# A pause of GpSimd at the end of a convolution block, and chunks of a normed input moved from ScalarE to VectorE

## What is computed

```
mod = silu(c) @ mod_w[layer] + mod_b[layer]          # 6 x 1024 columns
sh_m, sc_m, gt_m, sh_f, sc_f, gt_f = split(mod, 6)
h = x * (1 + sc_m) + sh_m                            # "normed input", modulated
y = concat(s5(h @ w_in), gla(h @ w_in)) @ w_out      # mixing block
x = layer_norm(ALPHA * x + (1 + gt_m) * y)
h = x * (1 + sc_f) + sh_f
f = swiglu(h)   (layer 0)   or   top-2 of 8 experts (layer 1)
x = layer_norm(ALPHA * x + (1 + gt_f) * f)
```

## Time and profile before

| | us |
|---|---|
| median of 3 runs | 2672.69 |
| lowest, highest | 2669.34, 2675.71 |
| the profiled execution | 2669.51 |
| its span in the profile | 2667.7 |

### The profile page before, as it was taken

How to read it: one execution, slowest core, us unless ns; L and a number is a source line. 1 busy time by engine, 2 the same in 40 slices (tenths; PEclk the granted TensorE clock), 3 DMA queues, 4 the chain that set the end, 5 groups by cost and what they waited for, 6 DMA issues and landing times. The chain is left out here.

```text
span 2667.7 us, 41694 instructions
## 1 busy us (share of the span) xinstructions
PE 2547.6 (95%) x15530; PEld 2223.3 (83%) x15530; DVE 2078.8 (78%) x2194; ACT 1495.0 (56%) x1786; POOL 902.1 (34%) x564
## 2 busy tenths in 40 slices
PE   8999899999998999988999887999999999999997
PEld 7999689999997999767999766888888888888885
DVE  6777666676788766787565787898989898989897
ACT  4336543343344343554343555777777777777775
POOL 6990069969859986023470020000000000000000
PEclk9999999999998999899999898999999999999999
DMA  8764357667656664325555325999999999999995
GB/s 304 258 236 157 113 213 258 230 215 257 236 203 228 226 211 166 123 88 189 182 180 182 119 92 215 350 360 333 366 341 359 347 353 353 351 353 351 349 345 187
DMA packets 214166, 665.31 MB, mean 249 GB/s; under 512 B 14640, under 2 KB 14960, under 8 KB 193952
## 3 DMA queue, kind: packets, MB, share of 16 engines
q1 hardware_dynamic: 196752, 602.62, 62.5%
q0 software_dynamic: 17296, 61.06, 6.7%
HBM read 662.58 MB, written 1.05 MB: 249 GB/s over the span
## 5 line engine op out<-in xcount | busy, mean ns | idle before, releaser
L1827 PE MATMUL work<-xT_hi,wh_gu 128*128 128x256 f32 x2088 | 595.3, 285 | 19.2 <-DVE xT_lo L1056 11.7
L1828 PE MATMUL work<-xT_lo,wh_gu 128*128 128x256 f32 x2088 | 593.3, 284 | 0.0
L1829 PE MATMUL work<-xT_hi,wl_gu 128*128 128x256 f32 x2088 | 592.7, 284 | 0.0
L924 DVE TENSOR_TENSOR wl_gu<-raw_gu,wh_gu 128x2048 fp32r<-128x2048 f32 x158 | 390.0, 2468 | 84.8 <-ACT wh_gu L407 84.4
L1827 PEld LDWEIGHTS work<-xT_hi,wh_gu 128*128 128x128 f32 x2088 | 402.5, 193 | 26.9 <-issue 20.8
L1828 PEld LDWEIGHTS work<-xT_lo,wh_gu 128*128 128x128 f32 x2088 | 402.9, 193 | 4.5
L1829 PEld LDWEIGHTS work<-xT_hi,wl_gu 128*128 128x128 f32 x2088 | 402.7, 193 | 0.0
L929 DVE TENSOR_TENSOR wl_d<-raw_d,wh_d 128x1024 fp32r<-128x1024 f32 x157 | 236.8, 1509 | 180.4 <-ACT wh_d L414 180.4
L1827 PE MATMUL acc<-wh_d,h_hi 128*128 128x512 f32 x912 | 371.5, 407 | 3.4 <-DVE h_lo L1529 2.7
L1828 PE MATMUL acc<-wl_d,h_hi 128*128 128x512 f32 x912 | 359.8, 395 | 0.0
L1829 PE MATMUL acc<-wh_d,h_lo 128*128 128x512 f32 x912 | 359.0, 394 | 0.0
(11 more groups left out here) (465 smaller groups left out, 4623.8 us busy)
## 6 DMA issues: line engine op xcount, KB each, us to landing
raw_gu<-in_w_gu SPq DMA_DIRECT2D x269, 1024.0 KB, 5.9
raw_d<-in_w_d SPq DMA_DIRECT2D x269, 512.0 KB, 5.2
scratch<-in_w_gu SPq DMA_DIRECT2D x112, 1024.0 KB, 7.5
scratch<-in_w_d SPq DMA_DIRECT2D x112, 512.0 KB, 6.7
scratch<-in_w_mod POOLq DMA_DIRECT2D x96, 512.0 KB, 3.6
rows<-in_norm_post POOLq DMA_DIRECT2D x6, 512.0 KB, 4.5
rows<-in_ln_g POOLq DMA_DIRECT2D x4, 512.0 KB, 4.3
rows<-in_ln_b POOLq DMA_DIRECT2D x4, 512.0 KB, 7.3
```

What stands on the lines that cost most here:

```text
L924: TT(wl, raw_gu[k][:, :], wh.bitcast(F32), ALU.subtract).then_inc(gu_lo, 1)
L1827: pe.matmul(out_, w[0], m[0], start=start, stop=False)
L1828: pe.matmul(out_, w[0], m[1], start=False, stop=False)
L1829: return pe.matmul(out_, w[1], m[0], start=False, stop=stop)
```

## The change

Three edits. GpSimd, in the fourth quarter of the modulation, waits before the 13th of its 24 steps until block 4 is done. In blocks 6, 7 and 8 chunk 1 is modulated by VectorE and no longer by ScalarE. The counts on `xt_f` and `xt_raw`, now three chunks each in a block, follow in ScalarE's `high` and in TensorE's waits of the last block; the last block itself keeps its shares (ScalarE 0, 1, 2 and 4, VectorE 3 and 5).

```diff
                 def high(j):
...
-                    if j in (3, 5):
-                        act.wait_ge(xt_raw, 2 * c + j // 2)
-                    else:
-                        act.wait_ge(xt_f, 4 * c + (1, 2, 3, 0, 4, 0)[j])
+                    act.wait_ge(xt_raw if j % 2 else xt_f, 3 * c + j // 2 + 1)
...
-                for j in (0, 1):
-                    modulated(j)
+                modulated(0)
                 if b == len(SUBS) - 1:
+                    modulated(1)
                     modulated(2)
                     modulated(4)
                     return
@@ gpsimd, modulation(i)
                     pool.wait_ge(mod_in[n % 3], 16 * (8 * i + n // 3 + 1))
+                    if i == 3 and n == 12:
+                        pool.wait_ge(x_done, SECOND - 1)
@@ tensor, moe(b)
-                    pe.wait_ge(xt_f, 4 * (b - SECOND) + (4 if t else 2))
+                    pe.wait_ge(xt_f, 3 * (b - SECOND) + (4 if t else 2))
                     if t:
-                        pe.wait_ge(xt_raw, 2 * (b - SECOND + 1))
+                        pe.wait_ge(xt_raw, 3 * (b - SECOND) + 2)
```

## The result

| | before | after |
|---|---|---|
| median of 22 runs each | 2674.22 us | 2676.74 us |
| lowest to highest | 2668.41 to 2678.44 | 2673.73 to 2680.78 |
| ratio of after to before, 95% interval | | 1.0015 (1.0008 to 1.0022) |
| the profiled execution | 2669.51 | 2677.67 |
| its span in the profile | 2667.7 | 2675.9 |

By the ratio the change costs 4 us (2 to 6); the two medians are 2.5 us apart. Either is less than the 0.2% that I had named as the least that can be told, though with this many runs its sign is clear. In the profile of after, lines of GpSimd, VectorE and ScalarE have numbers two or three lower than before (1094 for 1096, 1709 for 1711, 1758 is the same); TensorE's are the same.

What follows compares the result with a forecast made beforehand. TensorE, busy in 95% of the span, was taken to bound the kernel, with time won only in gaps between blocks. +7.2 us for block 5 and -3.2 us for three starts gave +4.0 on 2672.69: 2676.7 us, range 2668 to 2683.

Steps and rivals of the forecast that it cites:

- pause, end of block 4: End of block 4: VectorE's additions run undisturbed by GpSimd, so block 5's first matmul comes 2.4 us earlier (2.1 to 2.9).
- start of TensorE's turning of B, against before: Block 5: TensorE waits 7.7 us for B's loads and turns B at about 956.0 instead of 950.75, +5.3 us.
- clock behind the stand: Block 5, after TensorE's wait for B: 3 to 4.8 us at half speed, costing 1.9 us (1.4 to 2.4).
- three starts: Starts of blocks 6 to 8: with chunk 1 on VectorE, TensorE starts 1.07 us earlier each time, -3.2 us together.
- clock in blocks 6 to 8: First matmuls of these blocks run at half clock; where that ends decides the gain, -1.6 to -6 us.
- that may return: End of block 4: the diagonal can meet GpSimd's first product and lose about 0.8 us, partly hidden behind ScalarE's table load.
- GpSimd's delay: Modulation's fourth quarter: step 13 starts 8.0 us later, the last twelve steps take 86.2 us, the quarter ends 7.1 us later.
- The landing of B: Block 5: the last of B's eight transfers, issued at 949.2, lands 6.5 us later, at 955.7; ends 3.4 and 7.8 us.
- The stand of 3 us by the page's figure: Block 5: by the Trainium skill's fit alone, B is there at 951.4 and TensorE idles about 3 us.
- Line 1932: TensorE's next wait, at 1002.9: has room, everything later by the same 7 us within 2; a gap there would disprove the forecast.
- long stand: Rival, block 5: GpSimd needs 88.0 us, B takes 7.8 us, TensorE turns B at 959.1; +7.0 us, 2679.7; chance 0.20.

## Why the prediction came out, and what in it was wrong

I forecast 2676.7 us, and the median is 2676.74. That close a hit is luck: the terms were off by 0.6 to 1.4 us each, with both signs; the kernel before has a median of 2674.22 over 22 runs and not the 2672.69 of the three that I added to; and 2.1 us in the block of experts are in no term of mine. What the runs bear out is the mechanism, and a difference of 2 to 6 us.

| term | predicted | in the trace |
|---|---|---|
| pause, end of block 4 (contained in the next) | -2.4 | -1.84 |
| start of TensorE's turning of B, against before | +5.3 | +6.7 |
| clock behind the stand | +1.9 | +3.0 |
| three starts | -3.2 | -4.1 |
| clock in blocks 6 to 8 | in the range | -1.3 |
| sum | +4.0 | +4.3 |

- **The pause.** Right in its mechanism, but it left out TensorE's clock. Counted from block 4's last matmul, ScalarE's table load starts 2.87 us earlier (6.63 us for 9.50), which is what the additions had lost (2.89). Then ScalarE waits 0.51 + 0.56 us for turnings that run at the lower clock for 5.0 us, where it had waited 0.15, and 1.84 us arrive. The value lies under my lower bound of 2.1 by 0.3. The 0.8 us "that may return" with the diagonal did return in large part (0.95 us beside GpSimd's product, undisturbed 0.29), hidden behind the table load.
- **GpSimd's delay.** The best step: last twelve steps 86.2 us predicted, 86.2 measured. The last load of B was predicted at 949.2, or 951.2 with the 2.0 us by which this execution ran late; it was 951.1.
- **The landing of B.** I took 6.5 us, between 3.4 and 7.8, since the weight loads should be still. It was 8.3, outside both ends. This is the term that was sized worst. Those loads weren't still when the stand began: the DMA engines were full all through it (1.03), and the 512 KB of the gain stood ahead (B first: 6.7 us). With fewer weight loads beside it, in the run with the pause before step 12, the last landed in 4.3. The Trainium skill's DMA: Bandwidth & Descriptors, section "Anatomy of one DMA — SWDGE (gpsimd) path", by whose fit 64 KB take 2.2 us (an estimate from it: 2.0 us plus the bytes over 436 GB/s), agrees with the first load of B when nothing of GpSimd's is queued ahead of it (2.1 us, B ahead of the gain), and is far off for the last of eight under load. The stand of 3 us by the page's figure didn't come.
- **The start of the turning** is the sum of both: 959.44 - 2.0 - 950.75 = +6.7 us. It makes a stand of 8.09 us, predicted 7.7, TensorE having come later than I had it.
- **The clock.** I counted 3 to 4.8 us at half speed from a row in block 8; it was six. I took the row's 4.0 us as the whole, when it only says that the clock was at 0.50 up to its end (it came back at about 1581.4, after 4.4 us). Nor does the length of the stand tell it: behind stands of 5.93, 7.32, 8.09 and 12.46 us the clock stayed at 0.50 for 4.5, 3.3, 6.0 and 5.2 us. What sets it no run here shows; the six us of after are the longest of the four.
- **The chunks.** Sized too low by a third. I had put VectorE 0.2 us behind ScalarE; in the trace it is VectorE that waits 0.20 for ScalarE, and `low(2)` starts 1.32 us earlier, relative to ScalarE's first piece, not 1.07. The clock gave 1.3 us more, within my bounds, though part of that is the trace: with the old shares, too, the clock stayed low at the start of block 6 for 5.3 us in before and for 3.0 with the pause alone.
- **Line 1932** shows no wait of its own in after, as expected.

The errors add up to +1.4 + 1.1 - 0.9 - 1.3 = +0.3 us; by the lengths of whole blocks (+9.46 - 4.1 - 1.3) the sum is +4.1, and with the block of experts +6.2, the upper end of what the times allow. None of the rivals came true, though the "long stand" was nearest in the landing (7.8); it had GpSimd's end wrong (88.0 us for 86.2).

## What to carry to other kernels

A pause that takes one engine out of another's way can make everything behind it late; before making it, find the last load issued by that engine and how long before use it lands. Here that margin was 0.8 us, the pause made the loads 7 us late, and moving the reader by one pass of a loop, which by itself cost nothing (1.0001), made the difference between 1.0015 and 0.9969. Two edits in one change should be timed apart: this one hid a gain of 0.23% under a loss of 0.33%.

## What the runs showed of the hardware

- VectorE's addition to the residual took 3.23 us beside an addition of GpSimd's, 2.23 where it met one of its products, 1.28 alone; this was in the trace of before. There the second diagonal, beside an addition of GpSimd's, took 1.42 us, for 0.29 in after. That an operation as small as the diagonal loses 0.66 us (0.95 for 0.29) at the start of GpSimd's product and nothing 1.3 us later in the same product, I had not expected.
- The same loads of 64 KB landed in 2.1 us at the least with nothing of GpSimd's ahead of them, in 4.1 to 5.0 at the least behind 512 KB; the last of the eight took 4.3 us in one kernel, 6.7 and 6.9 in two, and 7.4 to 8.5 in the other eight.
- After a stand of 8.09 us TensorE had the granted clock 0.50 (1.2 GHz) for six us from its restart; over the three us from 965.00 on it was 0.92. Behind the three other stands it was 0.50 for 3.3 to 5.2 us, the least behind one of 7.32 us and not behind the shortest.
